# Routing of a mixture-of-experts stage: the list of the first sixteen chunks is made from the ranks alone, and the rest of the counting moves into later waits

## The reference

```python
lg = h @ w_group + b_group                 # 4 groups
gi = argmax(lg);  gw = max(softmax(lg))
le = (h @ w_expert + b_expert)             # 16 experts, 4 in each group
tv, ti = top_k(le of group gi, 2)          # two experts for each token
tw = softmax(tv) * gw
gate, up = split(h @ w1[e]);  y += tw_e * ((silu(gate) * up) @ w2[e])
x = x + gate2 * y
```

## Time and profile before

| | us |
|---|---|
| median of 3 runs | 1822.55 (1820.56 to 1829.57) |
| the profiled execution, its own time | 1825.2 |
| its span | 1823.3 |

### The profile page before, as it was taken

One profiled execution on the slowest core, in us unless ns is written; L12 is line 12 of the kernel. 1 busy time (PEld: TensorE's weight loads), 2 busy tenths in 40 slices (PEclk: granted clock), 3 DMA queues, 4 the chain that ended last, 5 costly groups with the idle time before them and its releaser, 6 DMA issues.

```text
span 1823.3 us, 34025 instructions
## 1 busy us (share of the span) xinstructions
PE 1624.9 (89%) x13197; PEld 1093.6 (60%) x13197; DVE 1158.3 (64%) x1859; ACT 892.2 (49%) x1477; POOL 494.4 (27%) x444
## 2 busy tenths in 40 slices
PE   5899989999989984988889998899999999489885
PEld 3478766777765553444466886677776655344444
DVE  4494355777636755887556926477774394768874
ACT  4322555666641232877543236466664312258763
POOL 0222243221231323222143315322212321133313
PEclk9899999999999996998979999999999999789998
DMA  9565535532336635999845542232223366489975
GB/s 325 176 212 173 170 133 184 195 111 73 100 124 218 210 128 197 364 380 374 321 157 172 193 155 92 79 103 76 73 77 122 129 213 231 146 293 340 402 293 197
DMA packets 191615, 351.33 MB, mean 193 GB/s; under 512 B 15795, under 2 KB 99314, under 8 KB 191218
## 3 DMA queue, kind: packets, MB, share of 16 engines
q1 hardware_dynamic: 182005, 320.17, 50.2%
q0 software_dynamic: 7776, 28.32, 4.3%
q10 hardware_dynamic: 1693, 0.89, 0.2%
HBM read 288.32 MB, written 61.01 MB: 192 GB/s over the span
## 4 chain that ended last, share of the span: by engine, by line
PE 66%; issue 8%; DVE 8%; DMA 7%; ACT 7%; POOL 1%; DVEq 1%; SPq 1%; POOLq 0%; ACTq 0%
PE PS L440 39%; PE PS L447 12%; PE PS L1176 3%; PE PS L1160 3%; DMA wf<-in_moe_w 3%; DMA arena<-in_moe_w 3%; PE PS L946 2%; ACT whi L1747 1%; PE PS L911 1%; PE PS L928 1%; ACT arena L1578 1%; DVE arena L2553 1%; DVE scratch L2499 1%; POOL wlo L1921 1%; DMA hpart<-y_rows,wulo 1%
## 5 line engine op out<-in xcount | busy, mean ns | idle before, releaser
L1870 POOL TENSOR_TENSOR wlo<-wf,whi 128x256 f16<-128x256 f32 (+1 forms) x276 | 294.7, 1101 | 850.7 <-ACT whi L1494 799.7
L440 PE MATMUL PS<-hpart,whi 128*128 128x320 f16 x2048 | 423.2, 300 | 19.0 <-ACT arena L1578 17.8
L440 PE MATMUL PS<-hpart,wlo 128*128 128x320 f16 x1024 | 306.4, 299 | 0.0
L440 PE MATMUL PS<-whi,hpart 128*128 128x256 f16 (+2 forms) x1536 | 286.3, 287 | 9.7 <-issue 5.9
L440 PEld LDWEIGHTS PS<-hpart,whi 128*128 128x128 f16 x2048 | 190.1, 98 | 108.7 <-issue 39.7
L440 PE MATMUL PS<-wlo,hpart 128*128 128x256 f16 (+2 forms) x768 | 218.7, 287 | 0.0
L440 PEld LDWEIGHTS PS<-whi,hpart 128*128 128x128 f16 x1536 | 148.4, 98 | 65.9 <-issue 28.0
L2365 DVE TENSOR_REDUCE stat<-PS 128x1 f32<-128x640 f32 (+1 forms) x160 | 110.7, 713 | 80.1 <-PE PS L1160 77.5
L447 PE MATMUL PS<-hpart,whi 128*128 128x128 f16 (+1 forms) x768 | 139.3, 305 | 12.4 <-DVE hpart L2040 10.8
L1578 ACT ACTIVATE arena<-PS,pcol 128x320 f32<-128x320 f32 x128 | 67.4, 527 | 168.1 <-PE PS L440 162.9
L2193 DVE SCALAR_TENSOR_TENSOR scratch<-scratch,cw 128x655 f32<-128x655 f32 x120 | 138.6, 1197 | 4.5
(11 more groups left out here) (361 smaller groups left out, 2858.7 us busy)
## 6 DMA issues: line engine op xcount, KB each, us to landing
arena<-in_moe_w SPq DMA_DIRECT2D x68, 1024.0 KB, 8.5
arena<-in_w_ada SPq DMA_DIRECT2D x48, 1024.0 KB, 7.9
wf<-in_w_gate SPq DMA_DIRECT2D x32, 1024.0 KB, 5.9
wf<-in_moe_w SPq DMA_DIRECT2D x32, 1024.0 KB, 9.6
g_rows<-arena SPq DMA_DIRECT2D x128, 160.0 KB, 1.8
wf<-in_w_in SPq DMA_DIRECT2D x18, 1024.0 KB, 9.6
y_rows<-scratch SPq DMA_DIRECT2D x34, 512.0 KB
arena<-g_rows SPq DMA_DIRECT2D x24, 640.0 KB, 5.2
```

Of the source, the lines that this page charges most:

```text
L440: ins = pe.matmul(out, st, mv, start=first and n == 0, stop=last and n == 2)
L1870: ins = pool.tensor_tensor(lo[:, a:b], wf[j][:, a:b], hi[:, a:b], ALU.subtract)
```

## The change

It does the following, with line numbers of the kernel before unless said otherwise.

1. DVE makes the list of chunks 0, 1 and 2 from the ranks alone: a rank below 128 is the row in chunk e. `exhot` (10 x 16, the one-hot expert times the token's number) takes the place of `chhot` there. DVE signals `place_ready`, PE multiplies (10 products of 16 columns), and DVE copies three columns of `idxall`.
2. What was ahead of that list is cut into four pieces: `chunks` (counting chunks), `slots` (chunk and row of each pair), `loops` (expert of each chunk, number of loops, `route_ready`) and `places` (`chhot` and `rowhot` for the whole list). They stand later in DVE's order. PE makes the whole list in `list_whole`, behind `turn_act` of chunk 0, and DVE copies it (`listed`) behind the first low part after `multiply` of chunk 0.
3. POOL waits for the whole list (`idx_all`) ahead of its loop, where it had the two low parts of chunk 1; DVE makes these low parts directly behind the copy of the three columns.
4. `cum`, `before` and `ones` for the counting products are f16; their making stands ahead of the output projection. Small arrays move from `scratch` to `biasf`.
5. PE has idle products: 16 behind the last transposes of the projection, 8 behind the counting products, and 10 (6 before) ahead of the first transposes of rows.

```diff
@@ PE
+                busy(16)
                 pe.wait_ge(*hot_ready(l, 1))
-                pe.matmul(bank(4)[:, 128:224], before, cumz, start=True, stop=False)
+                pe.matmul(bank(4)[:, 128:224], before16, cumz, start=True, stop=False)
...
+                busy(8)
                 pe.wait_ge(*place_ready(l, 1))
                 for n in range(10):
-                    ins = pe.matmul(bank(5)[:, 0:CHUNKS + 2], rowhot[:, n, :], chhot[:, n, :], start=n == 0, stop=n == 9)
+                    ins = pe.matmul(bank(5)[:, 0:EXPERTS], rowhot[:, n, :], exhot[:, n, :], start=n == 0, stop=n == 9)
                 ins.then_inc(list_done.sem, 1)
-                pe.wait_ge(*idx_ready(l, 1))
...
-                busy(6)
+                busy(10)
                 turn_rows(0, 0, 0, True)
                 busy(3)
                 gate_up(0, 0, range(3), True)
                 turn_rows(1, 1, 1)
                 gate_up(0, 0, range(3, KC))
                 turn_act(0, 0, True)
+                list_whole()
                 pe.wait_ge(started.sem, 1)
                 pe.wait_ge(*route_ready(l, 1))
@@ POOL
                 rows_from(xg[0], idxall[:, 2:3], xg_in[0])
-                for q in range(1, 3):
-                    pool.wait_ge(mw_hi.sem, past * 3 + (4 + q))
-                    if q == 2:
-                        pool.wait_ge(mw_lo2.sem, past + 1)
-                    part_low(q)
+                pool.wait_ge(*idx_all(l, 1))
@@ DVE
+                for ch in range(2):
+                    dve.tensor_tensor(exhot[:, 5 * ch:5 * ch + 5, :], ohm[:, 5 * ch:5 * ch + 5, :],
+                                      bc(tokid.rearrange("p (n o) -> p n o", o=1), [P, 5, EXPERTS]), ALU.mult)
                 dve.wait_ge(*cnt_done(l, 1))
...
+                for ch in range(2):
+                    picked(ch, ch, ranks)
+                dve.drain()
+                dve.tensor_reduce(rsel[:, 0, :], tbl[:, 0:160].rearrange("p (n e) -> p n e", n=10), AX_X, ALU.add)
+                dve.drain()
+                row_hot(rsel[:, 0, :]).then_inc(place_ready.sem, 1)
...
                 dve.wait_ge(*list_done(l, 1))
+                dve.tensor_copy(idxall[:, 0:3], bank(5, 3)).then_inc(idx_ready.sem, 1)
+                dve.wait_ge(mw_lo.sem, past * 2 + 3)
+                part_low(1, 1, 1, 5)
+                part_low(1, 1, 2, 6)
+                chunks()
...
                 rows_low(0, 0)
+                slots()
                 rows_low(1, 1)
+                loops()
+                places()
                 multiply(0, 0, True)
-                dve.wait_ge(mw_lo.sem, past * 2 + 4)
                 part_low(0, 0, 0, 7)
+                listed()
                 dve.wait_ge(*rexp_ready(l, 1))
```

More of the change, by code:

```diff
@@ L1263, in _, with busy @@
                 turn_x1(l, KC - 1)
+                def busy(n):
+                    for _ in range(n):
+                        pe.matmul(bank(7, 256), ones[:, :], xT[:, 0, 0:256], start=True, stop=True)
+                busy(16)
                 pe.wait_ge(started.sem, 1)
@@ L1916, in _ @@
                 pool.wait_ge(mw_lo.sem, past * 2 + 2)
[L1918 to L1925, removed]
+                for a in range(0, 2048, 1024):
+                    ins = pool.tensor_tensor(mwlo[3][:, a:a + 1024], mwf[3][:, a:a + 1024], mwhi[3][:, a:a + 1024], ALU.subtract)
+                ins.then_inc(mw_lo.sem, 1)
                 def rows_from(dst, index, done):
@@ L2653, in _ @@
-                incl = csum[0][:, 8:24]
[L2654 to L2666, removed]
+                def chunks():
+                    count(nch, totals, steps[:, 1:5], ALU.is_gt, EXPERTS, 4)
+                    if l + 1 < LAYERS:
+                        dve.memset(rprow[:, 31:96:32], 0.0)
+                    dve.tensor_copy(csum[0][:, 8:24], nch)
+                    dve.drain()
+                    for n, sh in enumerate((1, 2, 4, 8)):
+                        a, o = csum[n % 2], csum[1 - n % 2]
+                        dve.tensor_tensor(o[:, 8:24], a[:, 8:24], a[:, 8 - sh:24 - sh], ALU.add)
+                        dve.drain()
+                    dve.tensor_tensor(first, incl, nch, ALU.subtract)
+                    dve.drain()
+                    dve.tensor_scalar(incl, incl, float(EXPERTS), None, ALU.add)
@@ new lines, in slots @@
+                def slots():
+                    for n, (ch, row16) in enumerate((ch, by) for by in (first, iota[:, 0:EXPERTS]) for ch in range(2)):
+                        picked(n + 2, ch, bc(row16.rearrange("p (o e) -> p o e", o=1), [P, TILES, EXPERTS]))
+                    dve.drain()
+                    dve.tensor_reduce(rsel[:, 1:3, :].rearrange("p a b -> p (a b)"),
+                                      tbl[:, 160:480].rearrange("p (n e) -> p n e", n=20), AX_X, ALU.add)
+                    dve.drain()
+                    count(whole, rank, steps[:, 1:5], ALU.is_ge, 10, 4)
+                    dve.scalar_tensor_tensor(out=row, in0=whole, scalar=-float(P), in1=rank, op0=ALU.mult, op1=ALU.add)
+                    dve.tensor_scalar(rsel[:, 3, :], whole, 0.0, None, ALU.is_equal)
+                    dve.tensor_tensor(extra, whole, extra, ALU.add)
+                    dve.drain()
+                    dve.tensor_scalar(extra, extra, float(EXPERTS - 1), None, ALU.add)
+                    dve.drain()
+                    dve.tensor_tensor(expert, expert, extra, ALU.subtract)
+                    dve.drain()
+                    dve.tensor_tensor(expert, expert, rsel[:, 3, :], ALU.mult)
+                    dve.drain()
+                    dve.tensor_tensor(chunk, expert, extra, ALU.add)
+                    dve.drain()
+                    dve.scalar_tensor_tensor(out=slotf[:, :], in0=chunk, scalar=float(P), in1=row, op0=ALU.mult, op1=ALU.add)
@@ L2667, in _, with listed @@
+                def listed():
+                    dve.wait_ge(*list_all(l, 1))
+                    dve.tensor_copy(idxall[:, 3:], bank(5)[:, 3:CHUNKS + 2]).then_inc(idx_all.sem, 1)
+                incl = csum[0][:, 8:24]
                 rank, extra, expert = rsel[:, 0, :], rsel[:, 1, :], rsel[:, 2, :]
                 whole, row, chunk = rsel[:, 4, :], rsel[:, 5, :], rsel[:, 6, :]
-                count(whole, rank, steps[:, 1:5], ALU.is_ge, 10, 4)
-                dve.scalar_tensor_tensor(out=row, in0=whole, scalar=-float(P), in1=rank, op0=ALU.mult, op1=ALU.add)
@@ L2673, in _ @@
[L2673 to L2689, removed]
```

93 lines of the change are left out of this document (52 added, 41 removed).

## The result

| | us |
|---|---|
| changed kernel, median of 4 runs | 1832.9 (1832.59 to 1835.16) |
| kernel before, beside it | 1823.01 (1820.56 to 1829.57) |
| ratio | 1.0051, 95% interval 1.0028 to 1.0075 |
| profiled execution of the changed kernel | 1832.62, span 1830.7 |

What follows compares the result with a forecast made beforehand. Bound taken: each layer's chain from output projection through DVE's routing, POOL and the first gather. Terms summed to +3.7 us a layer, +7.4 for two, median 1822.55 to 1829.9 us; forecast's own range 1825.5 to 1833, overall range 1817 to 1835.

Steps and rivals of the forecast that it cites:

- first gather starts: POOL's first gather of rows after routing: starts earlier thanks to the early list, -2.2 us a layer.
- its time to PE's first rows: From the first gather's start to PE's first rows: taken over unchanged at 4.71 us.
- clock at the first rows: PE idles ahead of chunk 0's rows and its clock may fall: +0.6 us a layer, between 0 and 2.26.
- `multiply` late: DVE's `multiply` of chunk 0 queues behind `loops` and `places`, 4.5 us in 1.39 us of room: +3.1 us a layer.
- `turn_act`, whole list: Ahead of chunk 1: 0.2 us for slower transposes, 0.3 us for ten more small products, in each layer.
- clock behind it: PE's clock falls while waiting for `multiply`, slowing chunk 1's fifteen products: +1.7 us a layer; bounds 0 and 2.5.
- The hold of POOL: DVE's two low parts hold POOL's two additions ahead of the first gather, so the gain is 2.2 us, not 6.1.
- my three bounds: First gather's gain: 6.1 us if POOL slips through, 2.2 forecast, 1.5 if the indirect DMA is held once more.
- The gather's landing: From the first gather's start at 711.5 to its landing at 716.2, where PE gets its first rows.
- the case of the clock lost twice: Rival: PE's clock low through chunk 0's products and again behind `multiply`; +6.1 us a layer, 1834.8 us, chance 0.17.
- The stage that the weights pace: Later stage of each layer, behind the first chunks: claimed to carry a shift over and give nothing back.

Runs made afterwards that it cites:

- e1: Changed kernel with `chunks` ahead of DVE's two low parts of chunk 1 instead of behind them; 1823.31 us, ratio to before 0.9990.
- a0: The changed kernel itself, run again unchanged; 1835.39 us, ratio to before 1.0062.
- e2: Changed kernel with eight idle products on PE ahead of `turn_act` of chunk 0; 1830.07 us, ratio to before 1.0039.
- e3: Changed kernel with `slots` and `loops` ahead of the low part of chunk 0's rows, `places` ahead of that of chunk 1's; 1829.11 us, ratio 1.0026.
- e8: Changed kernel without the 16 and 8 idle products, with 6 instead of 10 ahead of the first rows; 1830.65 us, ratio to before 1.0058.
- e4: e1 plus, on DVE, `slots` ahead of chunk 0's rows, `loops` and `places` ahead of chunk 1's; 1818.69 us (0.9981), second trial 1818.83 (0.9975).
- e9: e4 with the count of loops behind the low part of chunk 1's rows; 1818.1 us, ratio to before 0.9976.
- e10: e9 with two idle products on PE ahead of `turn_act` of chunk 0; 1820.73 us, ratio to before 0.9985.
- e6: Changed kernel with chunk 1's low parts back on POOL behind its gathers, and e3's order on DVE; 1835.59 us, ratio to before 1.0079.

## Why the prediction came out as it did

The mechanism held, and the sum came near: 1829.9 us forecast for the median, 1832.9 measured; the changed kernel's profiled execution was forecast at 1832.6 us and took 1832.62. That last agreement is luck: I forecast the same +3.7 us for each layer, and by the marks one layer lost 2.2 us more and the other 1.2 us less. The terms show where (us in a layer, from the marks):

| step | forecast | layer 0 | layer 1 |
|---|---|---|---|
| first gather starts | -2.2 | -2.48 | -2.62 |
| its time to PE's first rows | 0 | +1.29 | -0.83 |
| clock at the first rows | +0.6 | +0.88 | +0.88 |
| `multiply` late | +3.1 | +3.54 | +3.07 |
| `turn_act`, whole list | +0.5 | +0.02 | +0.10 |
| clock behind it | +1.7 | +2.61 | +1.85 |
| sum | +3.7 | +5.86 | +2.45 |

*The hold of POOL* was right, in size and in place; e1 shows that the low parts cause it. Of my three bounds (6.1, 2.2, 1.5 us of gain) the middle one came true, and the indirect DMA itself was not held (1.11 us). Freed, the gather starts 6.23 and 5.77 us earlier than before, against 6.1 estimated.

*The gather's landing* I had taken over unchanged (4.71 us). In the five profiles in which the gather starts as in the changed kernel (that one, a0, e2, e3, e8), PE had its rows 6.0 to 6.6 us after its start in layer 0 and 4.4 to 4.7 in layer 1, where the kernel before had 4.76 and 5.33. The moment of the start doesn't settle it: in the five profiles in which the gather starts as in e1 (e1, both of e4, e9, e10) the time was 5.1 to 5.9 us in layer 0 and 4.3 to 4.8 in layer 1. What sets it wasn't tried.

*The clock at the first rows* stood at 0.50 (eight transposes 1.97 us instead of 1.09), and with the three idle products (six rows) behind them PE was busy until the clock came back, within the first of the nine products of chunk 0 (2.25 us, against 2.11 in e9), so that the case of the clock lost twice, which I gave 0.17, did not come.

*`multiply` late* was sized from rows of before, 4.5 us of work in 1.39 us of room, and e3 shows the cause. *`turn_act` and the list* were priced too high by 0.4 us: the ten products take 0.41 to 0.47 us, inside the 0.9 us that PE spends between `turn_act` and chunk 1's first product anyway. *The clock behind it* I had cut from 2.26 to 1.7 us for a share on the transposes; it cost 2.6 and 1.85, and the uncut row would have been nearer. e2 shows this term by itself.

*The stage that the weights pace* carried the shift over in these two profiles, as taken: from the mark to the gathers of the experts' results, at the layer's end, the changed kernel takes 5.1 and 2.5 us longer than before, 7.6 in sum against 8.3 us in the marks ahead of the stage. But it also wanders by up to 10 us by itself, more than any single term here; so single profiled spans (1809.7 for e10, 1830.7 for the changed kernel) say less than marks. The marks don't say all either. Over the twelve comparisons (the result, a0 and the ten others) the time, by its ratio to the kernel before, stands on average 3 us higher than the marks of both layers together, and only in e1 it doesn't: forecasts of a gain came out too good (e4: -8.2 us by the marks, -3.5 by the ratio). Either something outside the marks costs this, or the one profile of the kernel before, 2.65 us above its median, has late marks; that stays open.

## What to carry to other kernels

Before moving elementwise work to another engine to shorten a chain, look at what stands beside it in time: two long instructions with two SBUF inputs took 3.75 and 3.15 us of a gain of 6.2 and 5.8 us from two tiny additions of POOL, and 2.2 us of counting put ahead of them gave it back. Place displaced work by the idle time ahead of each wait, in us, not by which wait looks late: the same 4.5 us cost 3.3 us ahead of `multiply` and nothing when split over the two waits ahead of it. When a stage wanders by more than the change is worth, measure from a common mark inside the execution.

## What the runs showed of the hardware that was not expected

DVE and POOL did not take turns everywhere. At 678.8 us in the kernel before each lost 2.0 us to the other; in e6 four instructions of POOL in a row (8.4 us) kept one small instruction of DVE waiting for 8.84 us, though by its row it had started first (708.19 against 708.63), while the last gather's instruction was still on POOL. The Trainium skill (SBUF — State Buffer, "Who interferes with whom") says that the order of issue decides who is held; by the starts in these rows it didn't. What decides wasn't tried.

PE's clock fell also behind gaps under 1 us. The timeline of PE, e9, layer 0, and then of the kernel before at the same place:

```profile
723.23 0.44 PE L1334 MATMUL PS<-ident,scratch 128*128 128x128 f32 x2 [0.93 <-DVE scratch L2758]
723.50 0.41 PE L1298 MATMUL PS<-scratch 128*128 128x27 f16 x10
724.63 0.44 PE L444 MATMUL PS<-whi,hpart 128*128 128x512 f16 x1 [0.73 <-issue]
```

```profile
729.19 0.44 PE L1321 MATMUL PS<-ident,scratch 128*128 128x128 f32 x2 [0.93 <-DVE scratch L2714]
730.55 0.39 PE L440 MATMUL PS<-whi,hpart 128*128 128x512 f16 x1 [0.92 <-issue]
```

In e9 PE stood 0.93 us, made twelve small products, stood 0.73 us, and the granted clock went from 1.00 to 0.50 in the window at 725. The kernel before had two such gaps too, the second a little longer (0.92 us, 0.87 in layer 1), and kept the clock: its products took 3.24 us in both layers. e4 held the clock in layer 0 in one execution and lost it in another, with the same gaps; what tips it is open.
